# Where pair 0's third activation sum is kept, and the order of VectorE and ScalarE beside the first block pair of a Strassen FFN

## The reference

```python
h2 = rmsnorm(x, norm2_w)
gu = h2 @ w_ffn_up                     # 1024 -> 2 * 2816
x = x + (silu(gu[..., :D_FF]) * gu[..., D_FF:]) @ w_ffn_down
```

## Time and profile before

| what | value |
| --- | --- |
| median of 3 runs | 1685.45 us |
| profiled execution: its own time | 1684.72 us |
| its span, first to last instruction | 1683.0 us |
| mean granted TensorE clock | 0.996 |
| busy: PE, DVE, ACT, POOL | 98%, 57%, 33%, 47% |

### The profile page before, as it was taken

The page is one execution under the profiler, slowest core; times in us unless marked ns, Lnnn a source line. Parts: engine busy times, 40 slices in busy tenths (PEclk is TensorE's granted clock), DMA queues, the critical chain, the costliest instruction groups (busy, mean ns, idle before and its releaser), DMA issues. The chain is left out here.

```text
span 1683.0 us, 30880 instructions
## 1 busy us (share of the span) xinstructions
PE 1653.4 (98%) x12241; PEld 1604.5 (95%) x12241; DVE 965.2 (57%) x1642; ACT 556.0 (33%) x1240; POOL 791.2 (47%) x756
## 2 busy tenths in 40 slices
PE   7999999999999999999999999999999999999997
PEld 7999999999999998889899999999999999999997
DVE  6859811406534554777873289666665565744346
ACT  5332121342213332443411154444443333322233
POOL 5483122322321111141422325877777777787774
PEclk9999999999999999999999999999999999999998
DMA  5364363232233244434465431544333344966443
GB/s 209 82 129 131 105 198 103 89 92 91 87 93 102 89 130 141 153 118 138 132 212 191 159 119 46 182 157 148 147 141 141 141 168 167 365 225 267 162 188 104
DMA packets 95660, 245.85 MB, mean 146 GB/s; under 512 B 14352, under 2 KB 42000, under 8 KB 95272
## 3 DMA queue, kind: packets, MB, share of 16 engines
q1 hardware_dynamic: 73392, 174.08, 30.5%
q0 software_dynamic: 10256, 33.59, 6.6%
q10 hardware_dynamic: 11880, 36.36, 6.3%
HBM read 177.11 MB, written 66.65 MB: 145 GB/s over the span
## 5 line engine op out<-in xcount | busy, mean ns | idle before, releaser
L1636 PE MATMUL ps<-HL,WH 128*128 128x384 f32 (+1 forms) x1536 | 507.3, 330 | 4.3 <-DVE HL L689 1.8
L1637 PE MATMUL ps<-HH,WL 128*128 128x384 f32 (+1 forms) x1536 | 496.9, 324 | 0.0
L1638 PE MATMUL ps<-HH,WH 128*128 128x384 f32 (+1 forms) x1536 | 496.1, 323 | 0.0
L1636 PEld LDWEIGHTS ps<-HL,WH 128*128 128x128 f32 x1536 | 289.2, 188 | 15.5 <-issue 9.4
L1637 PEld LDWEIGHTS ps<-HH,WL 128*128 128x128 f32 x1536 | 289.4, 188 | 0.3
L1638 PEld LDWEIGHTS ps<-HH,WH 128*128 128x128 f32 x1536 | 289.2, 188 | 0.0
L1280 POOL TENSOR_TENSOR WL<-WRAW,WH 128x1024 fp32r<-128x1024 f32 x59 | 145.6, 2467 | 246.9 <-DMA WH<-in_w 246.9
L1277 POOL DMA_DIRECT2D WH<-in_w x59 | 34.5, 585 | 348.6 <-PE ps L1638 347.1
L2927 DVE TENSOR_TENSOR X<-X,ps 128x528 f32<-128x528 f32 (+2 forms) x170 | 107.8, 655 | 155.3 <-PE ps L2231 104.4
L2320 ACT ACTIVATE GT<-ps 128x384 f32<-128x384 f32 (+1 forms) x72 | 33.3, 464 | 214.7 <-PE ps L1638 177.5
L2927 DVE TENSOR_TENSOR RB<-RB,ps 128x528 f32<-128x528 f32 x60 | 42.1, 701 | 103.5 <-ACT RB L2842 86.0
(11 more groups left out here) (467 smaller groups left out, 4265.6 us busy)
## 6 DMA issues: line engine op xcount, KB each, us to landing
WRAW<-in_w SPq DMA_DIRECT2D x75, 512.0 KB, 3.3
ffn_scratch<-STG SPq DMA_DIRECT2D x70, 528.0 KB, 3.5
WH<-in_w POOLq DMA_DIRECT2D x62, 512.0 KB, 4.4
SOP<-ffn_scratch SPq DMA_DIRECT2D x36, 528.0 KB, 8.5
gate_scratch<-GT ACTq DMA_DIRECT2D x24, 528.0 KB, 3.4
PX<-gate_scratch ACTq DMA_DIRECT2D x22, 528.0 KB, 4.0
HL<-ffn_scratch SPq DMA_DIRECT2D x22, 528.0 KB, 10.5
RAWB<-in_w SPq DMA_DIRECT2D x10, 1024.0 KB, 6.2
```

The source lines that it names most:

```text
L1636: nc.tensor.matmul(out, wh, rl, start=start, stop=False)
L1637: nc.tensor.matmul(out, wl, rh, start=False, stop=False)
L1638: return nc.tensor.matmul(out, wh, rh, start=False, stop=stop)
```

## The change

For q = 0 the third sum goes to SX and no longer to the upper half of GT; its high and low part read it there. VectorE's order at x = 0 is written out anew: after the three sums come quadrant read 2, low part 0, read 3, read 4, the product of the lower half, read 5; then low parts 1 to 3, the last sum, low parts 4 to 6 and the product of the upper half. On ScalarE, high parts 4 and 5 of q = 0 move behind `weight_high(9)` and the SiLU of RG. GpSimd's first weight difference of block pair 1 waits for the three sums (`fs_ok`, 3) and no longer for four low parts (`fl_ok`, 4). All other block pairs keep their order.

```diff
+    def f_third(q):
+        return SX[:] if q == 0 else GT[:, UPPER]
     def f_source(q, i):
-        return (GT[:, LOWER], s_temp(q)[0], s_temp(q)[1], GT[:, UPPER], s_temp(q)[0], FODD[:, LOWER], FODD[:, UPPER])[i]
+        return (GT[:, LOWER], s_temp(q)[0], s_temp(q)[1], f_third(q), s_temp(q)[0], FODD[:, LOWER], FODD[:, UPPER])[i]
...
             if x == 1:
-                after(pool, fl_ok, 4)
+                after(pool, fs_ok, 3)
             difference(x, W12, W11, W11, 1, 0)
...
             weight_high(g + 8)
-            if q is not None:
+            if q is not None and q >= 1:
                 f_high(q, 4)
                 f_high(q, 5)
             weight_high(g + 9)
             silu(x, RG, 3)
+            if q == 0:
+                f_high(q, 4)
+                f_high(q, 5)
             if q is not None:
                 f_high(q, 6)
             weight_high(g + 10)
...
-                          (GT[:, UPPER], GT[:, LOWER], GT[:, UPPER], ALU.subtract))[i])
+                          (f_third(q), GT[:, LOWER], GT[:, UPPER], ALU.subtract))[i])
...
             quadrant(x, RV, R2, 5, 0)
             if q == 0:
                 f_sums(q)
+                after(dve, dr, 5 * x + 1)
+                after(dve, fs_ok, 3)
+                quadrant(x, f[:, UPPER], RV, 7, 1)
                 f_low(q, 0)
-                f_low(q, 1)
+                quadrant(x, RG, R1, 2, 2)
+                after(dve, fl_ok, 1)
+                quadrant(x, f[:, LOWER], R2, 3, 3)
+                after(dve, dr, 5 * x + 4)
+                ffn_product(x, LOWER, RG, 1)
+                after(dve, dr, 5 * x + 2)
+                quadrant(x, RV, R2, 4, 4)
+                for i in range(1, 4):
+                    f_low(q, i)
+                f_sum_last(q)
+                for i in range(4, 7):
+                    f_low(q, i)
+                ffn_product(x, UPPER, RV, 2)
+                continue
```

## The result

| | runs | median, us |
| --- | --- | --- |
| before | 7 | 1686.82 (1684.75 to 1688.70) |
| changed | 7 | 1690.86 (1690.11 to 1693.52) |

The ratio is 1.0027, 95% interval 1.0018 to 1.0037: slower by about 4.6 us (the medians are 4.0 apart). The profiled execution's span is 1689.3 us.

What follows compares the result with a forecast made beforehand. TensorE, busy 98% of the span, was taken as the bound. Two gaps won (-2.25, -0.93), a new stall (+5.7) and low clock (+2.2) sum to +4.7 us, median 1690.1; 8-in-10 range 1685.8 to 1693.2.

Steps and rivals of the forecast that it cites:

- Parts 1 and 2: TensorE's waits before product 4 of pair 0 and product 7 of pair 1 go: gains of 2.25 and 0.93 us.
- Part 3: Later low part 1 delays store 2, high part 6 and product 6 of pair 1: new stall 5.7 us (2.1 to 8.3).
- Part 4: TensorE's clock falls to the low level after the new stall, costing 2.2 us (ends 0 and 3.3).
- Rival B: The stall before product 6 of pair 1 comes but the clock stays up: +2.5 us, 1688.0; chance 0.16.
- The sum: Whole kernel: -2.25 - 0.93 + 5.7 + 2.2 = +4.7 us, median 1690.1.
- C: Store 2 lands in time and only the two gaps on TensorE go: -3.2 us, 1682.3; chance 0.12.
- D: Second stall at products 2 and 3 of pair 1, or later low part 1 and landing: +7 to +10, 1693.5; chance 0.12.

Runs made afterwards that it cites:

- e2: Changed kernel with the 1 MB load for pair 2 issued ahead of store 0 on SP's queue; pairs 0 and 1 45.08 us, ratio 1.0010.
- e8: Changed kernel with high parts 4 to 6 of q = 0 behind ScalarE's copy to R1 for pair 1; pairs 0 and 1 43.34 us, ratio 1.0003.
- e1: Changed kernel with 48 idle-filling matmuls on TensorE ahead of product 6 of pair 1, where it stalled; pairs 0 and 1 47.88 us, ratio 1.0021.
- e3: Kernel before with only the third sum in SX and read 2 right behind the three sums; pairs 0 and 1 44.67 us, ratio 1.0002.
- e5: Changed kernel with low parts 1, 2 behind low part 0, low part 3 behind read 3, load ahead of store 0; pairs 0 and 1 42.38 us, ratio 0.9989.
- e9: e7 with the product of the upper half (pair 0) ahead of low parts 4 to 6 on VectorE; pairs 0 and 1 40.84 us, ratio 0.9983.
- e7: e5 with high parts 4 to 6 of q = 0 behind ScalarE's copy to R1 for pair 1; pairs 0 and 1 42.08 us, ratio 0.9988.
- e10: Changed kernel itself again, second profile on another chip and more timed runs; pairs 0 and 1 49.64 us, ratio 1.0039.
- e4: Changed kernel with low parts 1 and 2 behind low part 0, low part 3 behind read 3, load not moved; pairs 0 and 1 43.34 us, ratio 1.0005.

## Why the prediction was right, by its steps

**Parts 1 and 2** held: 2.25 and 0.93 us were gained, read 2 ended 0.3 us ahead of its need (0.45 forecast) and read 5 at 1051.0 (1050.1 to 1051.3 forecast).

**Part 3** had the right chain and was 1.1 us short in size: a stall of 5.7 forecast, 6.8 measured. Low part 1 ended about 1052.1 where 1051.4 was taken, because it was held up beside GpSimd (it took 1.18 us, the next two low parts 0.70 each); store 2 landed 8.8 us after it (8.5 taken), at 1060.9; from high part 6's start to product 6 it was 1063.74 - 1060.99 = 2.75 (2.8 taken). e2 shows that the load in the queue makes 4.0 us of the stall, and e8 that it reaches product 6 only through ScalarE's order. ScalarE's wait was said to be 3 to 4 us and was 5.1, for the same lateness of store 2 as in the stall.

**Part 4**, the clock, was 2.2 us and measured 2.8 in one profile and 1.8 in the other. The figure was taken from 15 slow matmuls at the start of the run, where 28 and 17 came here, so that the order of size is earned and the nearness of the number is luck. e1 shows that idleness caused it. Rival B (the clock stays up) is refuted by both profiles. The rule cited from the Trainium skill ("TensorE: Matmul & The Clock Gate", Part 1, on the HAM clock gate), that an idle TensorE falls back to the lower level, agrees with them: 1.00 before the stall, 0.50 behind it. What the prediction left open is how short a wait suffices: e2's 2.7 us did, though the forecast of e2 had counted on the clock to stay up.

**The sum** was +4.7 us; in the profile it was -3.2 + 6.8 + 2.8 = +6.4, and the two pairs show 6.27. The two timed comparisons gave 4.6 and 6.6 us. So 4.7 was short of the profile by 1.1 us of stall and 0.6 of clock, and that it meets the first comparison almost to the tenth is luck. In the first comparison the timed runs' mean clock was mostly 0.995, above the profiled one's 0.993, so that they probably had less of the low clock behind the stall; that is argued from a rounded mean, not shown.

**Rivals C and D** did not come. C needed store 2 by 1057.4. D needed a second stall, and product 2 of pair 1 was not late. The low clock ahead of it is not needed to explain that: in e1, with the same stall and the clock at 1.00, product 2 starts 1069.17 - 1066.15 = 3.02 us behind product 6, without a wait. GpSimd's low part for it ends at 1068.89, 0.3 us ahead. So the margin was as narrow as forecast, and it held.

**Slips in the working.** One GpSimd operation stands between the low parts for products 6 and 2, not two; the sum was made with the right three operations, and from the start of the one to the end of the other it was 1066.42 - 1062.22 = 4.2 us (4.4 forecast). And the ends of the range are not what they are called: the middle of C and B is 1685.15 and not 1685.8, and D's low edge, 7 us over 1685.45, is 1692.5 and not 1693.2. The measured 1690.9 lies inside by either.

**Not in the prediction** was read 4: it had 0.8 us to spare before, so moving read 2 alone would have won nothing (e3).

## What to carry to other kernels

A wait in an engine's queue costs what stands behind it. When early work is put behind other work, follow its store, the transfers queued between, and the engine that waits for the slot, to the first thing behind that wait which the bound engine needs. A slack that exists only because of a stall earlier in the kernel is gone once that stall is mended, so a gain of 3.2 us has to be checked against everything with less slack than that. Here the first two moves, low parts 1 and 2 early and the load ahead of the stores, gave 1.9 us (e5). All of it came only in e9, which also has the waiting high parts behind the copy and the product of the upper half ahead of low part 4.

## What the runs showed of the hardware

The granted clock of a nearly always busy TensorE also fell with no wait before it. In e2, e7, e8, e9 and e10 there is a stretch at the low level near 386 us, which the kernel before (second fence) does not show; pair 0 starts 1.5 us later in four of them and 3.1 us later in e2, which has one more such stretch near 769 us. e10:

```profile
384.00:388.00 4.00, 4.00 (x26) 3.96 (x26) 0.83 (x5) 3.22 (x10) 0.63 (x2) 0.82 0.56 145
```

```profile
384.00:388.00 4.00, 4.00 (x30) 3.96 (x30) 0.83 (x5) 3.25 (x10) 0.64 (x2) 1.00 0.51 141
```

What stands right ahead of the fall is not a pause but small work: from 383.6 to 385.6 TensorE makes 18 matmuls of 8 columns on 16 rows, about 0.11 us apart, and the clock falls at 386.6. In e2 the fall near 769 comes behind 2 us of matmuls of 16 columns. The kernel before makes the same small matmuls at the same place and its clock stays up, so they do not bring it down each time; whether they are the cause, no run here tests.

e1 and e4 start pair 0 late (1030.1 and 1029.4) without such a stretch, so the clock is not the whole of it. But the two profiles of the changed kernel (the first and e10) differ by 1.5 us at pair 0's start, and by this stretch. So part of the scatter between runs of one kernel comes from the clock in places that no edit touched, and an edit of 3 us is read better in its own stretch than in the span.
